# State-space mixer, groups 0 to 2: the clamped differences of the backward direction on VectorE instead of ScalarE

## Chip, core and metric

One Trainium2 chip, one NeuronCore. The metric is the device time of one execution in microseconds (us). The engines are TensorE (PE, with PEld for its weight loads), VectorE (DVE), ScalarE (ACT), GpSimd (POOL) and SyncE (SP), which issues the DMAs. Each engine works through its own instructions in order and waits on semaphores where it needs another's result.

## What is computed

Two layers of a diffusion backbone run for 128 prompt and 512 sample tokens. Layer 0 is attention with pooling, layer 1 a bidirectional Mamba-2 state-space mixer (SSD); each is followed by a gated MLP. The change lies in the mixer, whose diagonal part per chunk of 128 tokens, group of 8 heads and direction is

```
acs = cumsum(dt * a)                                  # per chunk and head
lmat = exp(where(lower, acs[i] - acs[j], -inf))       # 128 x 128 per head
wmat = (C_i . B_j) * lmat * dt[j]
y_diag = wmat @ x
```

The backward direction is the same on the flipped sequence. There are 4 groups, 5 chunks (one of the prompt, four of the sample) and 2 directions.

## The kernel before

All products are fp32. For the large projections each weight tile is cut into a rounded part and a rest by GpSimd (L940 makes `w_hi`, L944 makes `w_lo`, each as two instructions of 128x512), and TensorE makes three products of them with the two parts of the input (L974). The in-projection of the mixer is 40 such tiles (e0 to e39), ten to a group: B, C, four tiles of x, four of z. The scan's work is put between them by a list written out by hand, `SSD`, which every engine walks through in the same order, each doing its own part of every event. So an event's place in the list is its place in each engine's queue.

Per chunk the list holds, among others: `seg` (the decay matrices), `cb` (the product C.B, and on VectorE its masking, L2381, the scaled inputs `xdt`, L2389, and the multiplication into the decay matrices, L2395), `csf`/`csb` (states), `yo` (the part from the state; TensorE L1400, VectorE L2298, L2407, L2409) and `yd` (the diagonal product on TensorE, L1383 and L1388, gated by VectorE in L2401). The projection tile of e on ScalarE and VectorE is L1718, L2317, L2318, L1721 for B, C and x (a conv of three taps, then SiLU) and L1709 for z. L1749 copies transposed x tiles out of PSUM. PSUM banks 4 to 7 are handed round: the use number u of the list may begin on TensorE when the use u - 4 has been read by ScalarE or VectorE (`ssd_begin`).

`seg` of a chunk works in place on a row buffer `R` (or `R_mid`, in turn; in the last group `R_last`), [128, 2 directions, 8 heads, 128]. A DMA (L849) puts the row acs[i] of each head on all partitions; it is issued once the diagonal product two chunks earlier has used the buffer. ScalarE then makes max(acs[j] - acs[i], 0) head by head (L1767, eight instructions of 128x128), waits for them, and makes exp(-x) over the whole direction (L1770, one instruction of 128x1024), first direction 0, then direction 1. VectorE has no part in `seg`. Chunk n = 5g + c; the first three groups are n < N_MID = 15.

In each group the neighbourhood of the five `seg` events is, in every queue:

- chunk 0: behind csb of chunk 3, ahead of csb of chunk 2
- chunk 1: behind cb and csf of chunk 0, ahead of z tile e9 of the group and of yd of chunk 0; on ScalarE the copy-out of e9 (L1709) follows, for which VectorE's L2401 waits
- chunk 2: behind yd of chunk 1, ahead of the next group's C tile and yo of chunk 2
- chunk 3: behind the next group's first x tile, ahead of yd of chunk 2
- chunk 4: behind cb and csf of chunk 3, ahead of a copy-out of transposed x (L1749), of the next x tile, and of yd of chunk 3 and yo of chunk 4

Of the kernel before, what the change touches and what calls it, by code (L numbers as in the profile page):

```python
# [19 lines left out]
ALU = mybir.AluOpType  # L20
ACT = mybir.ActivationFunctionType
# [11 lines left out]
CHUNKS = 1 + NS // P  # L33
# [8 lines left out]
GH = 8  # L42
# [202 lines left out]
def build(nc, A, O):  # L245
    with ExitStack() as ctx:
# [140 lines left out]
        dt, acs, dec, wst, eacs = (a(n, [P, CHUNKS, 64]) for n in ("dt", "acs", "dec", "wst", "eacs"))  # L387
# [18 lines left out]
        N_MID, N_ALL = CHUNKS * (GROUPS - 1), CHUNKS * GROUPS  # L406

        def row_home(n):

            if n < N_MID:  # L410
                return (R, R_mid)[n % 2]
            return (R, R_last)[(n - N_MID) % 2]
# [5 lines left out]
        def rows_in(n, d_):  # L418

            if n < N_MID:  # L420
                return (R_in, RM_in)[n % 2][d_], 16 * (n // 2 + 1)
            i = n - N_MID
            return (RL_in[d_], 16 * (i // 2 + 1)) if i % 2 else (R_in[d_], 16 * (-(-N_MID // 2) + i // 2 + 1))
# [44 lines left out]
        def sem(name):  # L468
            return ctx.enter_context(nc.semaphore(name))
# [91 lines left out]
        xw_done = sem("xw_done")  # L561
        st_done = sem("st_done")
        seg_exp = sem("seg_exp")
        W_done = sem("W_done")
        y_done = sem("y_done")

# [887 lines left out]
        def _(act):  # L1454
            A_ = nc.scalar.activation
# [5 lines left out]
            for s_, name in enumerate(("c_ctx", "c")):  # L1461
                ins = A_(svec[:, :, s_], par[:, PARAM_AT[name]:PARAM_AT[name] + KD], ACT.Silu)
# [55 lines left out]
            for ev in ATT:  # L1518
                kind = ev[0]
                if kind == "mm":  # L1520
                    _, t, q = ev
                    if q == 3 and t < 12:
                        h, i = divmod(t, 3)
                        act.wait_ge(*acc_free(t))
                        buf = (q_raw, k_raw, v_raw)[i]
                        for s_, cols in SEGS:
                            ins = A_(buf[:, cols], buf[:, cols], ACT.Identity, bias=buf[:, NP_ + s_:NP_ + s_ + 1])
# [15 lines left out]
                elif kind == "S":  # L1543
                    _, h, j = ev
                    n = 5 * h + j
                    for c in range(2):
# [5 lines left out]
                        i = 24 + 2 * (j % 2) + c  # L1552
                        A_(prob[j % 2][:, c, 0:P if j == 0 else KEYS], src, ACT.Exp, bias=small[:, i:i + 1],
                           scale=SCALE, accum_out=small[:, i + 4:i + 5]).then_inc(att_free_act, 1)
                elif kind == "T":
                    _, h, j = ev
                    b = att_wait(ev)
                    n = CHUNKS if j else 1
# [105 lines left out]
            for k in range(KD):  # L1664
                act.wait_ge(t_done, k + 1)
                for s_, cols in SEGS:
                    ins = A_(h_hi[:, k, cols], tn[k % 2][:, cols], ACT.Identity, bias=modc(1, 0, k, s_))
# [29 lines left out]
            for ev in SSD:  # L1697
                kind = ev[0]
                if kind == "mm":
                    _, e, q = ev  # L1700
                    if q == 0:
                        continue
                    what, m = ssd_tile(e)
                    g, i = divmod(e, 10)
                    act.wait_ge(mm_done, T_E + e + 1)
                    if what == "z":
                        if e == 36:
                            act.wait_ge(ssd_mm, SSD_USE[("yd", GROUPS - 2, 3)] + 1)
                        A_(yg[:, m, :], acc(e % 2), ACT.Silu).then_inc(acc_free_act, 1)  # L1709
                        continue  # L1710
                    if i < 2 and g >= 2:
                        act.wait_ge(*ssd_end(("yd", g - 2, 4)))
                    if i == 2 and g:
                        act.wait_ge(*ssd_end(("trx", g - 1, 3, 1)))
                    if i > 2:
                        act.wait_ge(*ssd_end(("trx", g, i - 3, 1)))
                    buf = conv_buf(e)
                    A_(buf[:, :], acc(e % 2), ACT.Identity, bias=conv_row("ssd_conv_b", m),  # L1718
                       scale=conv_row("ssd_conv_w", 24 + m)).then_inc(conv_id, 1)
                    act.wait_ge(acc_free_dve, dve_accs(A_E + e))  # L1720
                    A_(buf[:, :], buf[:, :], ACT.Silu).then_inc(conv_silu, 1)  # L1721
                    continue
                g = ev[1]
                if kind == "ynorm":
                    y_high(ev[2])
                elif kind == "dtT":
                    act.wait_ge(dt_xb, 1)
                    step(A_(dt_e, dt_x, ACT.Abs))
                    step.wait()
                    A_(dt_e, dt_e, ACT.Exp, scale=-1.0).then_inc(dt_exp, 1)  # L1730
                elif kind == "acsT":
                    act.wait_ge(tot_w, 1)
                    A_(eacs[:, :, :], acs[:, :, :], ACT.Exp)
                    A_(dec[:, :, :], dec[:, :, :], ACT.Exp)
                    A_(wst[:, :, :], wst[:, :, :], ACT.Exp).then_inc(acs_exp, 1)
                    for i in range(2):
                        b = ssd_wait(ev + (i,))
                        A_(acsT[:, 512 * i:512 + 128 * i], bank(b, 512 - 384 * i)[0:64, :], ACT.Copy
                           ).then_inc(ssd_free_act, 1)
                elif kind in ("trB", "trx"):  # L1740
                    for i in range(2):
                        b = ssd_wait(ev + (i,))
                        cs = slice(1, CHUNKS) if i == 0 else slice(0, 1)
                        dst = b_tok[g % 2][:, cs, :] if kind == "trB" else \
                            x_tok[g % 2][:, cs, ev[2] * P:(ev[2] + 1) * P]
                        if g >= 2 and i == 0 and (kind == "trB" or ev[2] == 0):
                            act.wait_ge(*ssd_end(("yd", g - 2, 4)))
                            act.wait_ge(st_done, CS_AT[("csf", g - 2, 3)] + 1)
                        A_(dst, bank(b, P * (4 if i == 0 else 1)).rearrange("p (c n) -> p c n", n=P), ACT.Copy  # L1749
                           ).then_inc(ssd_free_act, 1)  # L1750
                elif kind == "init":
                    d_ = ev[2]
                    b = ssd_wait(ev)
                    if g:
                        act.wait_ge(ssd_mm, SSD_USE[("yo", g - 1, 4, 1)] + 1)
                    A_(st_f[1][:, :] if d_ == 0 else st_b[:, 3, :], bank(b), ACT.Copy).then_inc(ssd_free_act, 1)
                elif kind == "seg":
                    n = 5 * g + ev[2]
                    c = ev[2]


                    for d_ in range(2):
                        act.wait_ge(*rows_in(n, d_))
                        R_ = row_home(n)
                        for r in range(GH):
                            i = 32 * d_ + GH * g + r
                            ins = A_(R_[:, d_, r, :], R_[:, d_, r, :], ACT.Relu, bias=acs[:, c, i:i + 1], scale=-1.0)  # L1767
                        step(ins)
                        step.wait()
                        A_(R_[:, d_, :, :], R_[:, d_, :, :], ACT.Exp, scale=-1.0).then_inc(seg_exp, 1)  # L1770
                elif kind == "stT":
                    for d_ in range(2):
                        b = ssd_wait(ev + (d_,))
                        if g or d_:
                            act.wait_ge(st_stored, 16 * (2 * g + d_))
                        A_(st_out[:, :, :], bank(b).rearrange("p (q n) -> p q n", q=4), ACT.Copy
                           ).then_inc(ssd_free_act, 1)
# [9 lines left out]
            for hi, i, _, _, k0, k1 in H2_PADS:  # L1787
                ins = A_(hi[:, i:i + k1 - k0, PADS], mod[:, 72 + k0:72 + k1, :], ACT.Copy)
# [11 lines left out]
        def _(dve):  # L1800
            tt, ts, stt, cp = nc.vector.tensor_tensor, nc.vector.tensor_scalar, nc.vector.scalar_tensor_tensor, \
# [143 lines left out]
            for ev in ATT:  # L1945
                kind = ev[0]
                if kind == "mm":
# [4 lines left out]
                    if t < 12:  # L1952
                        h, i = divmod(t, 3)
# [11 lines left out]
                    else:  # L1965
# [10 lines left out]
                        for d_ in range(g + 1):  # L1976
                            r = 1 << d_ >> 1
# [60 lines left out]
                elif kind == "S":  # L2038
                    _, h, j = ev
                    for c in range(2):  # L2040
                        b = att_wait(ev + (c,))
                        src = bank(b, P) if j == 0 else bank(b, KEYS, 512 - KEYS // 2)
                        i = 24 + 2 * (j % 2) + c
# [5 lines left out]
                elif kind == "mix":  # L2049
                    _, h, j = ev  # L2050
                    n = P if j == 0 else KEYS
                    i = 28 + 2 * (j % 2)
# [23 lines left out]
                elif kind == "rbO":  # L2076
# [4 lines left out]
                    for s_, cols in RANGES:  # L2081
                        rbp = bank(b, P) if s_ == 0 else bank(b + 1)
                        ins = stt(o_nrm[:, cols], o_sb[:, cols], small[:, 22:23], rbp, ALU.mult, ALU.mult)
# [134 lines left out]
            for k in range(KD):  # L2218
                if k >= 2:
                    dve.wait_ge(*h_done(2, k - 2))  # L2220
                for s_, cols in RANGES:
                    rbp = bank(4, P) if s_ == 0 else bank(5)
                    ins = stt(tn[k % 2][:, cols], xT[:, k, cols], gain1[:, 2, k, s_:s_ + 1], rbp, ALU.mult, ALU.mult)
# [78 lines left out]
            for ev in SSD:  # L2302
                kind = ev[0]
                if kind == "mm":
# [4 lines left out]
                    g, i = divmod(e, 10)  # L2309
# [33 lines left out]
                    continue  # L2343
                if kind == "ynorm":
                    y_low(ev[2])
                if kind in ("ynorm", "yout", "seg"):
                    continue
                g = ev[1]
                c = ev[2] if len(ev) > 2 else 0
# [4 lines left out]
                elif kind in ("csb", "csf"):  # L2354
                    if kind == "csb" and c == 4:
                        dve.wait_ge(*ssd_end(("init", g, 1)))
                    d_ = 0 if kind == "csf" else 1
# [18 lines left out]
                elif kind == "cb":  # L2376
                    n = 5 * g + c
# [14 lines left out]
                    for d_ in range(2):  # L2392
                        dve.wait_ge(seg_exp, 2 * n + d_ + 1)
                        R_ = row_home(n)
# [7 lines left out]
                elif kind == "yo":  # L2402
                    y_ = y1[c % 2][:, :]
                    chain(skip_term(g, c))
                    for d_ in range(2):
# [3 lines left out]
                        ins = tt(y_, y_, y2[:, :], ALU.add)  # L2409
# [22 lines left out]
            for hi, i, lo, j, k0, k1 in H2_PADS:  # L2432
                ins = tt(lo[:, j:j + k1 - k0, PADS], mod[:, 72 + k0:72 + k1, :], f32(hi[:, i:i + k1 - k0, PADS]),
                         ALU.subtract)
                (step(ins) if k1 < 7 else ins.then_inc(shift_lo, 1))
            for m in range(KD):
                dve.wait_ge(mm_done, so_done(m))
                buf = tn[m % 2]
                for s_, cols in RANGES:
                    ins = stt(buf[:, cols], acc(so_slot(m))[:, cols], modc(1, 2, m, s_), rbs[:, cols], ALU.mult, ALU.mult)  # L2440
# [79 lines left out]
```

## Time and profile before

| | us |
|---|---|
| median of 3 runs | 2003.85 (2001.09 to 2008.55) |
| the profiled execution | 1999.62 |
| its span of instructions | 1997.7 |
| TensorE busy | 1864.4 (93%) |
| VectorE busy | 1032.1 (52%) |
| ScalarE busy | 605.8 (30%) |
| GpSimd busy | 1194.4 (60%) |
| mean granted TensorE clock | 0.977 of full |

The first three groups' scan lies between 960 and 1290 us of the span, one group to some 109.5 us, and the three look alike. The rows below are of the middle one, group 1, about 1075 to 1185 us. In a timeline, the first number is the start, the second the time taken by the x instructions that the row merges, and the bracket the engine's idle time just before with what ended it.

### The profile page before, as it was taken

What the parts mean: (1) busy time and instruction counts of PE and PEld (TensorE: products, weight loads), DVE (VectorE), ACT (ScalarE), POOL (GpSimd) and SP (SyncE); (2) the same over time, 40 slices, a digit from 0 to 9 for tenths busy, and PEclk for the clock granted to TensorE, in tenths of its full rate; (3) what the DMA queues carried; (4) which work ended last, traced back from release to release, by engine and by line L of the source; (5) the groups of instructions that cost most, each with busy time, mean ns of one, the idle gap of its engine ahead of it and who ended that gap; (6) DMA issues with size and microseconds to landing.
All of it is one profiled execution on the core that took longest, in us unless ns stands there. A gap on an engine that the chain in (4) does not pass through costs nothing. (4 is left out here: it accounts for less than half of the span.)

```text
span 1997.7 us, 33452 instructions
## 1 busy us (share of the span) xinstructions
PE 1864.4 (93%) x12857; PEld 1757.2 (88%) x12857; DVE 1032.1 (52%) x1608; ACT 605.8 (30%) x1152; POOL 1194.4 (60%) x869
## 2 busy tenths in 40 slices
PE   3988879999999999999999999987899999999997
PEld 2867768999999999989989898976899999999997
DVE  4545566466236515546565656578335632661553
ACT  4224322122002202223665555575112210220221
POOL 2423325777767777665645455532787777777764
PEclk9989989999999999999999999998999999999999
DMA  8631413342424333351523333222322222222212
GB/s 291 216 99 42 134 35 129 121 156 74 149 65 161 112 116 128 120 174 43 152 93 109 114 107 97 91 90 82 98 75 63 73 74 74 74 73 69 73 56 76
DMA packets 256187, 208.65 MB, mean 104 GB/s; under 512 B 7352, under 2 KB 235741, under 8 KB 255453
## 3 DMA queue, kind: packets, MB, share of 16 engines
q1 hardware_dynamic: 256093, 207.32, 32.9%
q8 instruction: 69, 1.13, 0.2%
q14 instruction: 25, 0.20, 0.0%
HBM read 196.63 MB, written 10.67 MB: 104 GB/s over the span
## 5 line engine op out<-in xcount | busy, mean ns | idle before, releaser
L940 POOL TENSOR_SCALAR w_hi<-raw 128x512 fp32r<-128x512 f32 (+1 forms) x432 | 644.9, 1510 | 778.1 <-PE ps L974 710.8
L944 POOL TENSOR_TENSOR w_lo<-raw,w_hi 128x512 fp32r<-128x512 f32 (+1 forms) x432 | 556.3, 1308 | 0.0
L974 PE MATMUL ps<-h_hi,w_hi 128*128 128x320 f32 (+1 forms) x1688 | 414.3, 326 | 4.7 <-DVE h_lo L2214 3.1
L974 PE MATMUL ps<-h_lo,w_hi 128*128 128x320 f32 (+1 forms) x1688 | 391.1, 312 | 0.0
L974 PE MATMUL ps<-h_hi,w_lo 128*128 128x320 f32 (+1 forms) x1688 | 389.9, 311 | 0.0
L974 PEld LDWEIGHTS ps<-h_hi,w_hi 128*128 128x128 f32 x1688 | 286.9, 192 | 27.2 <-issue 22.7
L974 PEld LDWEIGHTS ps<-h_hi,w_lo 128*128 128x128 f32 x1688 | 287.2, 190 | 0.0
L974 PEld LDWEIGHTS ps<-h_lo,w_hi 128*128 128x128 f32 x1688 | 286.9, 190 | 0.2 <-issue 0.2
L2109 DVE SCALAR_TENSOR_TENSOR xT<-ps,mod,xT 128x128 f32 (+1 forms) x112 | 56.5, 546 | 269.0 <-PE ps L974 263.3
L974 PE MATMUL ps<-g_hi,w_hi 128*128 128x322 f32 (+1 forms) x816 | 188.8, 313 | 7.0 <-DVE g_lo L2170 7.0
L974 PE MATMUL ps<-g_lo,w_hi 128*128 128x322 f32 (+1 forms) x816 | 187.5, 311 | 0.0
L974 PE MATMUL ps<-g_hi,w_lo 128*128 128x322 f32 (+1 forms) x816 | 187.1, 310 | 0.0
L1639 ACT ACTIVATE cg<-ps,small,par 128x130 f32<-128x130 f32 x88 | 49.8, 616 | 374.6 <-DVE small L2154 374.6
L974 PEld LDWEIGHTS ps<-g_hi,w_hi 128*128 128x128 f32 x816 | 137.1, 189 | 9.2 <-DVE g_lo L2170 7.8
L974 PEld LDWEIGHTS ps<-g_hi,w_lo 128*128 128x128 f32 x816 | 137.8, 189 | 0.0
L974 PEld LDWEIGHTS ps<-g_lo,w_hi 128*128 128x128 f32 x816 | 137.5, 189 | 0.0
L1892 DVE TENSOR_TENSOR ps<-ps,rbs 128x642 f32<-128x642 f32 x88 | 72.9, 829 | 85.1 <-PE ps L974 85.0
L1639 ACT ACTIVATE cv<-ps,small,par 128x130 f32<-128x130 f32 x88 | 49.7, 616 | 210.5 <-DVE small L2154 210.5
L974 PE MATMUL ps<-h_c,w_hi 128*128 128x322 f32 (+1 forms) x440 | 101.4, 312 | 0.0
L974 PE MATMUL ps<-h_b,w_hi 128*128 128x322 f32 x352 | 81.6, 314 | 0.0
L974 PE MATMUL ps<-h_b,w_lo 128*128 128x322 f32 x352 | 81.2, 312 | 0.0
L974 PE MATMUL ps<-y_hi,w_hi 128*128 128x322 f32 (+1 forms) x256 | 62.2, 325 | 17.8 <-POOL w_lo L944 17.8
(343 smaller groups left out, 2827.7 us busy)
## 6 DMA issues: line engine op xcount, KB each, us to landing
raw<-in_ffn_w_up SPq DMA_DIRECT2D x88, 512.0 KB, 3.8
ada<-in_ada_w SPq DMA_DIRECT2D x36, 1024.0 KB, 6.3
raw<-in_ssd_w_in SPq DMA_DIRECT2D x40, 512.0 KB, 4.0
raw<-in_ffn_w_down SPq DMA_DIRECT2D x32, 512.0 KB, 3.9
ada_att<-in_ada_w SPq DMA_DIRECT2D x12, 1024.0 KB, 8.3
R<-scr_acs SPq DMA_DIRECT2D x22, 512.0 KB, 5.6
raw<-in_att_w_in SPq DMA_DIRECT2D x16, 512.0 KB, 7.1
raw<-in_ssd_w_out SPq DMA_DIRECT2D x16, 512.0 KB, 4.0
```

The lines of the kernel that those rows point to most:

```text
L940: nc.gpsimd.tensor_scalar(w_hi[j % 2][:, a_:b_, :], raw[j][:, a_:b_, :], 1.0, None, ALU.mult).then_inc(w_hi_done, 1)
L944: ins = nc.gpsimd.tensor_tensor(w_lo[j % 2][:, a_:b_, :], raw[j][:, a_:b_, :], w_hi[j % 2][:, a_:b_, :].bitcast(F32), ALU.subtract)
L974: ins = mm(out[:, cols], w[slot][:, k, :], x[:, cols], start=first and k == 0 and i == 0, stop=last and k == n - 1 and i == 2)
L1639: ins = A_(buf[:, cols], acc(half)[:, cols], ACT.Identity, bias=small[:, b_:b_ + 1], scale=param_at(m + (wc + 44)))
L1892: step(tt(acc(slot), acc(slot), rrow(n)[:, :], ALU.mult))
L2109: ins = stt(x_, acc(slot)[:, cols], gate, x_, ALU.mult, ALU.add)
```

## The change

For n < N_MID, in direction 1 only, the eight clamped differences move from ScalarE to VectorE, as min(acs[i] - acs[j], 0), and ScalarE's exponential loses its scale of -1. VectorE makes them at the `seg` event's place in its own queue, after waiting for the row's DMA, and signals `seg_diff`; ScalarE waits for that ahead of its second exponential. Direction 0 and the last group are as before.

```diff
@@ scalar engine, kind == "seg"
                     for d_ in range(2):
                         act.wait_ge(*rows_in(n, d_))
                         R_ = row_home(n)
+                        if d_ and n < N_MID:
+                            act.wait_ge(seg_diff, n + 1)
+                            A_(R_[:, d_, :, :], R_[:, d_, :, :], ACT.Exp).then_inc(seg_exp, 1)
+                            continue
                         for r in range(GH):
                             i = 32 * d_ + GH * g + r
                             ins = A_(R_[:, d_, r, :], R_[:, d_, r, :], ACT.Relu, bias=acs[:, c, i:i + 1], scale=-1.0)
@@ vector engine
-                if kind in ("ynorm", "yout", "seg"):
+                if kind == "seg":
+                    n = CHUNKS * ev[1] + ev[2]
+                    if n < N_MID:
+                        dve.wait_ge(*rows_in(n, 1))
+                        R_ = row_home(n)
+                        for r in range(GH):
+                            i = 32 + GH * ev[1] + r
+                            ins = ts(R_[:, 1, r, :], R_[:, 1, r, :], acs[:, ev[2], i:i + 1], 0.0, ALU.subtract, ALU.min)
+                        ins.then_inc(seg_diff, 1)
+                    continue
+                if kind in ("ynorm", "yout"):
                     continue
```

## Rows read from the trace of the kernel before

**Rows 1.** The page: busy time, share of the span, number of instructions.

```profile
PE 1864.4 (93%) x12857; PEld 1757.2 (88%) x12857; DVE 1032.1 (52%) x1608; ACT 605.8 (30%) x1152; POOL 1194.4 (60%) x869
```

**Rows 2.** By stretch: busy PE, PEld, DVE, ACT, POOL; clock; DMA share; GB/s.

```profile
960.00:1290.00 330.00, 323.24 (x2299) 291.29 (x2298) 206.26 (x279) 195.19 (x390) 172.71 (x120) 0.98 0.36 110
```

**Rows 3.** Waits of TensorE, 1080 to 1190 us: total, times, longest.

```profile
PE ps L1375 <- DVE y L2407: 1.3, 1, 1.3
PE ps L1369 <- DVE y L2407: 1.0, 1, 1.0
```

**Rows 4.** Timeline of ScalarE, group 1, chunk 2.

```profile
1120.18 2.43 ACT L1767 ACTIVATE R_mid<-R_mid,acs 128x128 f32<-128x128 f32 x8
...
1123.61 0.87 ACT L1718 ACTIVATE cT<-ps,par 128x642 f32<-128x642 f32 x1
```

**Rows 5.** Timelines of VectorE, TensorE and GpSimd behind it.

```profile
1124.51 0.88 DVE L2317 SCALAR_TENSOR_TENSOR cT<-ps,par,cT 128x641 f32<-128x641 f32 x1 [6.40 <-ACT cT L1718]
...
1126.23 0.90 DVE L2298 TENSOR_TENSOR y<-x_tok,d_bc 128x512 f32<-128x512 f32 x1
...
1128.00 0.46 PE L1375 MATMUL ps<-cT,bT 128*128 128x128 f32 x2 [1.25 <-DVE y L2407]
...
1124.05 2.54 POOL L944 TENSOR_TENSOR w_lo<-raw,w_hi 128x512 fp32r<-128x512 f32 x2
```

**Rows 6.** Prices: a group of VectorE by form, then timelines of VectorE and GpSimd.

```profile
L2059 DVE TENSOR_SCALAR att<-prob,small 128x128 f32<-128x128 f32 x4 | 1.1, 279 | 0.0
...
917.65 2.95 POOL L940 TENSOR_SCALAR w_hi<-raw 128x512 fp32r<-128x512 f32 x2 [4.06 <-PE ps L974]
...
919.17 0.73 DVE L2252 TENSOR_SCALAR R<-R 128x320 f32<-128x320 f32 x1
...
922.25 1.31 DVE L2242 TENSOR_SCALAR R<-R 128x320 f32<-128x320 f32 x1
...
924.12 0.33 DVE L2242 TENSOR_SCALAR R<-R 128x320 f32<-128x320 f32 x1
```

**Rows 7.** The row buffer `R_mid`: its DMAs, issue to landing.

```profile
DMA to landing us min/median/max: 3.6/5.6/10.6
```

**Rows 8.** Timelines at chunks 0 and 3 of group 1: VectorE's idle time.

```profile
1085.38 0.90 DVE L2372 TENSOR_TENSOR y<-st_b,dec 128x512 f32<-128x512 f32 x1 [2.25 <-PE ps L1369]
...
1143.18 0.69 DVE L2401 TENSOR_TENSOR yg<-ps,yg 128x512 f32<-128x512 f32 x1 [3.80 <-PE ps L1388]
```

**Rows 9.** Timelines of ScalarE, VectorE and GpSimd at chunk 1 of group 1.

```profile
1094.65 1.07 ACT L1770 ACTIVATE R<-R 128x1024 f32<-128x1024 f32 x1
...
1098.09 1.06 ACT L1770 ACTIVATE R<-R 128x1024 f32<-128x1024 f32 x1
...
1100.46 0.71 ACT L1709 ACTIVATE yg<-ps 128x642 f32<-128x642 f32 x1
...
1098.65 0.06 DVE L2368 MEMSET small<- 128x1 f32 x1
...
1101.27 0.69 DVE L2401 TENSOR_TENSOR yg<-ps,yg 128x512 f32<-128x512 f32 x1 [2.56 <-ACT yg L1709]
...
1098.16 2.94 POOL L940 TENSOR_SCALAR w_hi<-raw 128x512 fp32r<-128x512 f32 x2 [3.01 <-PE ps L974]
```

**Rows 10.** The same engines and TensorE at chunk 4 of group 1.

```profile
1156.26 1.06 ACT L1770 ACTIVATE R_mid<-R_mid 128x1024 f32<-128x1024 f32 x1
...
1160.65 0.74 ACT L1749 ACTIVATE x_tok<-ps 128x512 f32<-128x512 f32 x2
...
1159.23 0.06 DVE L2375 MEMSET small<- 128x1 f32 x1
...
1161.43 1.02 PE L1400 MATMUL ps<-st_b,cT 128*128 128x512 f32 x2
...
1157.94 3.30 POOL L940 TENSOR_SCALAR w_hi<-raw 128x512 fp32r<-128x512 f32 x2 [2.32 <-PE ps L974]
...
1161.21 2.52 POOL L944 TENSOR_TENSOR w_lo<-raw,w_hi 128x512 fp32r<-128x512 f32 x2
```

More of the change, by code:

```diff
@@ L563, in build @@
         seg_exp = sem("seg_exp")
+        seg_diff = sem("seg_diff")
         W_done = sem("W_done")
```

## The prediction, made before the changed kernel was run

> **What bounds the kernel now.** The page first: TensorE is busy 93% of the span, the others 30 to 60% [rows 1]. So the question is what TensorE waits for where the change lies. The busy times by stretch say how much there is to win: in the 330 us of the three groups it works 323.24 us, idle 6.8 us in all [rows 2]. ScalarE is busy 195.19 of 330 us there, VectorE 206.26: neither is full, and VectorE, which gets the work, is the fuller one. The waits of TensorE in one group then say where the idle time is: two waits of 1.3 and 1.0 us, both for VectorE's L2407 [rows 3], and the same two stand in each group, 3 x 2.25 = 6.8 us, all of it. I call this place the seam. The timelines give the chain into it: ScalarE makes chunk 2's `seg`, direction 1's differences 1120.18 to 1122.61 among it, and only then begins the C tile at 1123.61 [rows 4]; VectorE, idle for 6.40 us, follows with L2317 at 1124.51, L2318, L2298, L2407, and TensorE, which needs the PSUM bank of L2407, starts at 1128.00 after 1.25 us of idling [rows 5]. Whoever reads no further expects 2.4 us off this chain and up to 2.25 us back per group.
>
> **What is removed.** Eight L1767 per chunk, 2.43 us [rows 4], 15 x 2.43 = 36 us of ScalarE's time. It counts only where TensorE waits for ScalarE. The SiLU and Exp tables are loaded as before: the differences of direction 0 and both exponentials remain.
>
> **What is added: the price.** Eight VectorE instructions of 128x128 per chunk, one input, a scalar per partition. The nearest row is L2059, same form, 279 ns [rows 6]; in the timeline such neighbours overlap by some 0.08 us, so I take 0.2 us each and 1.4 + 0.28 = 1.7 us for eight. GpSimd's splitting can hold them up. Of the same operation on 128x320, which takes 0.33 us alone (at 924.12), one takes 1.31 under a GpSimd L944 (at 922.25), and one 0.73 under an L940 (at 919.17) [rows 6]: an L944 instruction holds it for up to its own 1.27 us, half of its row of 2.54 for two [rows 5], an L940 for 0.40. From above: all eight held by 0.4 is 1.7 + 3.2 = 4.9 us and more if L944 joins. From below 1.7, since no row of this form is quicker than 279 ns; below nothing it can't be, for VectorE gives up no work. I take two holds per chunk where an L940 runs, 1.7 + 0.8 = 2.5 us, since most VectorE work under L940 goes at its own pace; both ends stay for the range. The Trainium skill, page "SBUF — State Buffer", section "Who interferes with whom", says that a VectorE instruction of this kind and a GpSimd instruction exclude each other for the whole instruction. The trace agrees for L944 and not for L940, where 0.40 us was waited of 1.47, half its row of 2.95 [rows 6].
>
> **What is added: the waits.** VectorE waits for the row's DMA. The load goes out after the diagonal product two chunks earlier and lands within 10.6 us [rows 7], and VectorE reaches `seg` 17 us or more after that product's end (least at chunk 4: 1142.1 to 1159.3); ScalarE never waited for it in these groups. Cost nothing; if a load came late, all of VectorE's queue would stand behind it. ScalarE waits for `seg_diff`, and behind that wait stands its next copy-out. This is what decides, so I go through the five places of a group, asking when VectorE gets there and when ScalarE wants the result (the end of its first exponential).
>
> Chunk 0: VectorE is there at 1082.5, and idles 2.25 us soon after [rows 8]; with L944 in the way the eight end at about 1086.6. ScalarE wants them at 1085.5, and is done at 1087.7 where it was done at 1089.0. Nothing behind it is hurt. Chunk 2: VectorE is there at 1118.1, inside its idle 6.40 us [rows 5], ScalarE at 1120.3. Hidden. Chunk 3: there at 1139.4, inside an idle 3.80 us [rows 8], wanted at 1144.9. Hidden, L944 included.
>
> Chunk 1: ScalarE's first exponential ends at 1095.72, but VectorE is there only at 1098.71, behind the previous chunk's L2395, L2289 and L2366 [rows 9]. ScalarE stands idle until VectorE has done, 1098.75 + 2.5 = 1101.2. Exponential 1.06, the table load in the 1.3 us between it and L1709, L1709 0.71: that ends at 1104.3, where it ended at 1101.17 [rows 9], and L2401 on VectorE, which waits for it, starts 3.1 us late. VectorE had some slack: 0.49 us idle ahead of L2381, and 0.58 us that L944 had cost it and no longer does. It loses 0.4 to an L940 later. The B tile's conv and SiLU ahead of chunk 2 come some 2.4 us late. That is just the 2.43 us which chunk 2's `seg` has lost on ScalarE: the C tile starts when it did, and **the seam stays**, 0 us. And small gains would not show: L2298 at 1126.23 already waits for L944's second instruction to end [rows 5], so the C tile must come 0.9 us earlier before any of it reaches TensorE. A loss does show, less 0.2 us.
>
> Chunk 4: ScalarE's first exponential ends at 1157.32, VectorE is there at 1159.29, under L940, with L944 from 1161.21 [rows 10]. Differences until 1159.3 + 2.5 = 1161.8, exponential until 1162.9; before, the copy-out L1749 behind it started at 1160.65, now at 1162.85, 2.2 us later. TensorE's L1400 at 1161.43 uses the PSUM bank that this copy-out frees at 1161.23 [rows 10]: slack 0.2. So **TensorE gets a new stall of 2.0 us**, once per group. What follows (the x tile, L2401, L2407) is late by 2.2 with TensorE late by 2.0, within the 0.3 us of slack that the next bank has; nothing gives the 2.0 back, since TensorE has no idle time until the next group's seam, whose chain hangs on TensorE itself.
>
> **The sum.** Seam 0, stall +2.0, three groups: +6 us. On the profiled execution 1999.62 + 6 = 2006; on the median, 4.2 above it, 2003.85 + 6 = 2010.
>
> **Rivals.**
> - Forecast, 0.58: 2010. Its own range: with one hold at chunk 4 the stall is 1.6 and the sum 5; with two holds and 0.4 us more in chunk 1, the seam adds 0.2. 2007 to 2013.
> - The last differences of chunk 4 fall behind L944, 0.17. Decides at 0.1 us: the eighth would start at about 1161.1 with one hold, L944 at 1161.21 [rows 10]. Then +1.25 per group on top, 3 x 3.3 = 10 us, and with 0.6 us of loss at the seam 2014 to 2016.
> - GpSimd holds nearly every difference, 0.12. One difference, one GpSimd instruction in turn: at chunk 4 three instructions (L940's second, both L944) of 1.5 + 2.5 us, so that the differences end at 1165.5, stall 5.6; at chunk 1 four of them, 4.2 us beyond my 1101.2, all of it at the seam. 3 x 9.8 = 29 us, 2033. For it: L944 does so [rows 6]. Against: L940 gave way after 0.40 us. This is what the quoted page's rule gives if it holds for L940 too.
> - Hidden after all, 0.08: VectorE reaches chunks 1 and 4 earlier than now, since its waits for ScalarE's conv tiles shorten. Against: it is the split at L944 and TensorE that set its time there. Time 2004.
> - Faster, 0.05: VectorE's part of chunk 1 comes no later than ScalarE wants it, 1095.7, that is 3 us earlier than its row shows; then the C tile gains its 2.43 us and the seam goes, 3 x 2.25 = 6.8 us, 1997; to decide for it, chunk 4 must be free too.
>
> **The numbers.** About 0.5% (10 us) is what a measurement of this kernel can tell from no change. Likeliest 2010. The range takes in the rival of L944 and the hidden case, and some of the way to the case of 2033, whose price can come in part: 2001 to 2022. Below 1993.8: 0.03. Above 2013.9: the rival of L944 mostly, the 2033 case, and a little of the forecast's upper end: 0.31. Within: 0.66.
>
> **What the changed profile would show.** ScalarE idle ahead of its second exponential in chunks 1 and 4 of each group, 5 and 4 us, released by VectorE's differences, and in no other chunk for over 1.5 us. A new wait of TensorE's L1400 for ScalarE's L1749, 2 us, once per group. The seam's two waits of 1.3 and 1.0 us still there. Eight differences in 1.7 us where no GpSimd instruction runs, 2.5 under L940. The stretch of the three groups 6 us longer, the rest unchanged. The forecast is wrong if the L1400 wait is absent, if the seam is gone, or if the differences take over 3.5 us.

## The result

The changed kernel takes 2016.28 us (median of 6 runs, 2013.01 to 2018.18) against 2003.39 us for the kernel before in the same comparison. The ratio is 1.0063, with a 95% interval of 1.0051 to 1.0076: slower by 10 to 15 us. The likeliest forecast was 2010, the range 2001 to 2022.

The page of the changed kernel, busy times, answers to [rows 1]:

```profile
PE 1872.8 (93%) x12857; PEld 1764.6 (88%) x12857; DVE 1074.1 (53%) x1728; ACT 570.3 (28%) x1032; POOL 1196.2 (59%) x869
```

ScalarE has lost 120 instructions and 35.5 us, VectorE has gained 120 and 42 us. TensorE has the same instructions and is busy 8.4 us longer, since some of its matmuls ran slower; only about 2 us of that lie in the three groups' scan, the rest in code ahead of it and behind it that is the same. Its waits in the stretch of one group (1080 to 1195 us; total, times, longest) answer to [rows 3]:

```profile
PE ps L1401 <- ACT x_tok L1750: 2.7, 1, 2.7
PE ps L1376 <- DVE y L2422: 1.3, 1, 1.3
PE ps L1370 <- DVE y L2422: 1.0, 1, 1.0
```

The two waits of the seam are untouched. The new one, TensorE's L1401 (L1400 before) for ScalarE's copy of transposed x (L1750, before L1749), stands in each of the three groups, 2.7 or 2.8 us. Chunk 4 of group 1 in the timelines of ScalarE, VectorE, TensorE and GpSimd, with the idle time ahead of an instruction in brackets, answers to [rows 10]:

```profile
1160.81 1.06 ACT L1775 ACTIVATE R_mid<-R_mid 128x1024 f32<-128x1024 f32 x1
1167.30 1.06 ACT L1768 ACTIVATE R_mid<-R_mid 128x1024 f32<-128x1024 f32 x1 [5.43 <-DVE R_mid L2358]
1168.27 0.75 ACT L1750 ACTIVATE x_tok<-ps 128x512 f32<-128x512 f32 x2
...
1163.74 0.66 DVE L2358 TENSOR_SCALAR R_mid<-R_mid,acs 128x128 f32<-128x128 f32 x1
1163.76 0.06 DVE L2390 MEMSET small<- 128x1 f32 x1
1163.94 3.27 DVE L2358 TENSOR_SCALAR R_mid<-R_mid,acs 128x128 f32<-128x128 f32 x7
...
1168.90 2.08 PE L1401 MATMUL ps<-st_b,cT 128*128 128x512 f32 x2 [2.75 <-ACT x_tok L1750]
1169.98 1.52 PE L975 MATMUL ps<-h_hi,w_hi 128*128 128x322 f32 x2
...
1162.49 3.37 POOL L941 TENSOR_SCALAR w_hi<-raw 128x512 fp32r<-128x512 f32 x2 [2.34 <-PE ps L975]
1165.84 2.51 POOL L945 TENSOR_TENSOR w_lo<-raw,w_hi 128x512 fp32r<-128x512 f32 x2
```

Read it in this order. ScalarE's first exponential ends at 1161.87. VectorE begins the differences only at 1163.74 and needs until 1167.21, 3.47 us, since it shares that time with both kinds of GpSimd's split instructions. ScalarE has idled for 5.43 us when it makes the second exponential, and its copy frees TensorE's bank 2.75 us too late. Then there is something that the waits don't list: the pair of L1401 that took 1.02 us before [rows 10] takes 2.08, and the next pair of the projection 1.52 where it took 0.85. That pair in the kernel before:

```profile
1161.89 0.85 PE L974 MATMUL ps<-h_hi,w_hi 128*128 128x322 f32 x2
```

The granted clock, in stretches laid about this spot, goes with it. Columns: stretch, its length, busy time of PE, PEld, DVE, ACT, POOL, then the clock, the DMA share and GB/s. First the kernel before, then the changed one, both from the start of that L1400 or L1401:

```profile
1161.40:1165.00 3.60, 3.60 (x22) 3.12 (x22) 2.55 (x4) 2.91 (x3) 2.33 (x2) 1.00 0.46 176
```

```profile
1168.90:1172.90 4.00, 4.00 (x13) 2.97 (x14) 2.84 (x4) 3.02 (x4) 0.00 (x0) 0.61 0.50 137
```

At a mean of 0.61, most of the 4 us went at the lower of TensorE's two levels, 1.2 GHz, after a pause of 2.75 us. Laying the two traces of TensorE side by side, instruction by instruction, the lag behind the kernel before grows by 2.9 us at the wait and by another 1.6 us over the matmuls behind it, 4.5 us at each chunk 4.

Some of it comes back at the seam, where the pause is as long as it was. The kernel before, then the changed one, on TensorE:

```profile
1129.45 2.04 PE L1369 MATMUL ps<-xw,b_tok 128*128 128x512 f32 x2 [0.99 <-DVE y L2407]
1131.29 1.77 PE L1406 MATMUL ps<-consts,st_p 128*128 128x128 f32 x8
```

```profile
1135.65 1.10 PE L1370 MATMUL ps<-xw,b_tok 128*128 128x512 f32 x2 [0.99 <-DVE y L2422]
1136.58 1.04 PE L1407 MATMUL ps<-consts,st_p 128*128 128x128 f32 x8
```

The kernel before ran these at the lower level, the changed one not, in groups 1 and 2: 1.6 and 1.4 us less. In all, the three groups' scan has become 3 x 4.5 - 3.0 = 10.5 us longer. The two profiled executions differ by 14.6 us; of the other 4.1, 1.7 had arisen before the scan and 2.2 arose in the last 60 us, in code that is the same. These last 2.2 us are no effect of the change: all of the traces below but that of chunk 1 alone show them too against this one trace of the kernel before, also those of kernels that take the same time as it. 10.5 alone lies inside the interval of the ratio.

### The profile page after: what moved, and what is told of

The parts are those of the page before. It is cut to its first block and busy times, and to the rows that moved or that the text cites. A ratio compares the mean times of both kernels' runs of the same rounds, so it can differ in the third digit from the quotient of the medians.

```text
span 2012.2 us, 33467 instructions
## 1 busy us (share of the span) xinstructions
PE 1872.8 (93%) x12857; PEld 1764.6 (88%) x12857; DVE 1074.1 (53%) x1728; ACT 570.3 (28%) x1032; POOL 1196.2 (59%) x869
## 5 line engine op out<-in xcount | busy, mean ns | idle before, releaser
L945 POOL TENSOR_TENSOR w_lo<-raw,w_hi 128x512 fp32r<-128x512 f32 (+1 forms) x432 | 556.3, 1309 | 0.0
```

What stands on the lines that cost most here:

```text
L945: ins = nc.gpsimd.tensor_tensor(w_lo[j % 2][:, a_:b_, :], raw[j][:, a_:b_, :], w_hi[j % 2][:, a_:b_, :].bitcast(F32), ALU.subtract)
```

## The experiments

All but the last vary in which chunks of a group get the new division of work, and where in VectorE's queue. They share one form: a list of chunks, and the differences in a function. In short, against the changed kernel:

```diff
+        ON_DVE = [n for n in range(N_ALL) if n < N_MID and n % CHUNKS in (0, 1, 2, 3)]
-                        if d_ and n < N_MID:
-                            act.wait_ge(seg_diff, n + 1)
+                        if d_ and n in ON_DVE:
+                            act.wait_ge(seg_diff, ON_DVE.index(n) + 1)
...
-                    if n < N_MID:
-                        ...
+                    if n in ON_DVE:
+                        differences(n)
```

The ratios are to the kernel before, run beside each of them.

### Chunks 0 to 3, and chunk 4 alone

The diff above is the first; in the second the list is (4,).

> VectorE makes the differences in chunks 0 to 3 of a group, ScalarE in chunk 4 as in the kernel before. Theory: the loss is the meeting at chunk 4, where VectorE comes late and TensorE waits 2.8 us per group and then goes on at half clock for some us. So here the time is that of the kernel before, 2002 to 2005 us, TensorE's wait for ScalarE's transposed x copy is gone, and the seam's two waits of 1.3 and 1.0 us are still there, since chunk 1 still gives back what chunk 2 saves. Rival: the loss is VectorE's 42 us of new work and its contest with GpSimd, spread over all chunks alike: four fifths of 10.6 us stay, about 2012 us.

> The opposite: VectorE makes the differences in chunk 4 alone. Theory: all of the loss is there, 10 to 13 us over the kernel before, 2013 to 2017 us, with the wait of 2.8 us per group and the slow clock behind it. Rival (spread work): a fifth of 10.6 us, about 2005.5 us.

Without chunk 4: 2002.98 us, ratio 0.9985 (0.9971 to 0.9999); the wait of L1401 is gone and TensorE's waits in the group are those of before:

```profile
PE ps L1377 <- DVE y L2439: 1.3, 1, 1.3
PE ps L1371 <- DVE y L2439: 1.0, 1, 1.0
```

Chunk 4 alone: 2019.77 us, ratio 1.0058 (1.0037 to 1.0078), at least as slow as the whole change, with one chunk in five. The median lies above the 2013 to 2017 that were expected, 16 us over that of the kernel before; the ratio makes it 7 to 16 us. Four chunks of work on VectorE cost nothing that can be measured (in the trace the scan is as long as before, to 0.1 us), one costs it all. The theory of work spread evenly falls.

The second one's wait is longer than in the changed kernel, which was not expected:

```profile
PE ps L1402 <- ACT x_tok L1751: 3.9, 1, 3.9
```

Its differences there took from 1171.83 to 1175.80, 3.98 us, two of them held behind GpSimd's second kind of split instruction and not one, and VectorE came to them 0.7 us later against TensorE. In this trace, of the slowest of seven executions, the three groups' scan is 19 us longer than before: 4 us of waiting at each chunk 4, and 1.6 to 2.7 us of slow matmuls behind it.

### Without chunk 1, and without chunks 1 and 4

The lists are (0, 2, 3, 4) and (0, 2, 3).

> All chunks but chunk 1. Theory: without the meeting at chunk 1 the conv of the B tile isn't late, chunk 2 is 2.4 us shorter on ScalarE, and the seam's waits of 2.3 us per group go (6.8 us in all, and with them what the clock loses behind them, 1 to 1.5 us per group), while the stall of chunk 4 stays: 10.6 less 7 to 11 us, 2003 to 2007 us. Rival (spread work): four fifths of 10.6 us, about 2012 us, seam unchanged.

> Chunks 0, 2 and 3 only. Theory: neither meeting hurts, and the seam is gone: 7 to 11 us under the kernel before, 1992 to 1997 us. Rival (spread work): three fifths of 10.6 us, about 2010 us. A third view, that GpSimd's split pins VectorE's L2303 at the seam whatever comes before it: no gain, 2003 us.

Without chunk 1: 2006.00 us, ratio 1.0002 (0.9984 to 1.0019). TensorE has one wait left in the group, that of chunk 4:

```profile
PE ps L1402 <- ACT x_tok L1751: 2.7, 1, 2.7
```

The seam is gone, and with it 2.4 us of waiting and, in these traces, 1.4 to 1.7 us of slow matmuls per group: 12.0 us for the three groups. Chunk 4 costs 12.2 us in them, so the two cancel here too.

This trace also shows that a pause of 2.75 us doesn't always bring the slow matmuls. It is as long in all three groups. From the start of the L1402 behind it, group 0 and group 1:

```profile
1054.65:1058.65 4.00, 4.00 (x12) 2.97 (x13) 2.84 (x4) 3.02 (x4) 0.00 (x0) 0.57 0.47 133
1164.90:1168.90 4.00, 4.00 (x23) 3.52 (x24) 2.84 (x4) 3.02 (x4) 0.00 (x0) 1.00 0.47 131
```

In group 1 the clock stays up, and the loss behind the pause is 0.1 us; in groups 0 and 2 it is 1.7 us each.

Without chunks 1 and 4 there is no wait of TensorE in the group at all, and the kernel takes 1993.30 us, ratio 0.9930 (0.9909 to 0.9951). This is the gain that a first look at the seam promises. The view that GpSimd's split pins VectorE there whatever comes falls: it would have hidden 0.9 us, and the gain on the chain was 2.4.

### Chunk 2 alone, and chunk 1 alone

The lists are (2,) and (1,).

> VectorE makes the differences of chunk 2 alone, one chunk in five. Theory: chunks 0 and 3 are hidden on both engines and chunk 2 carries all of the gain, so the time is that of the kernel with chunks 0, 2 and 3: 1992 to 1996 us, no wait of TensorE left in the three groups. Rival (ScalarE's relief counts wherever it falls): a third of that kernel's gain of some 10 us, 2000 us.

> Chunk 1 alone. Theory: ScalarE waits there for VectorE, the B tile's SiLU comes 2 to 2.5 us late, and with chunk 2 as in the kernel before nothing pays it back: the seam's idle time grows from 2.3 to 4.5 us per group, some 7 us and up to 2 us of slow clock on top: 2009 to 2013 us. Rival: VectorE's slack takes it up, and the seam stays because GpSimd's split pins it: 2003 us.

Chunk 2 alone: **1991.52 us, ratio 0.9939 (0.9927 to 0.9952)**, the same gain as with chunks 0, 2 and 3 within the intervals, so chunks 0 and 3 do nothing that these times can tell. (In the traces the scan with chunks 0, 2 and 3 is 1.3 us the shorter, 0.4 us at each chunk 4.) It beats both kernels. Its stretch of the three groups, to be laid beside [rows 2], and the meeting at chunk 2 on ScalarE and VectorE:

```profile
960.00:1290.00 330.00, 329.47 (x2371) 298.55 (x2370) 216.07 (x309) 190.33 (x371) 180.08 (x126) 1.00 0.37 113
```

```profile
1118.08 1.06 ACT L1776 ACTIVATE R_mid<-R_mid 128x1024 f32<-128x1024 f32 x1
1119.05 1.04 ACT L1769 ACTIVATE R_mid<-R_mid 128x1024 f32<-128x1024 f32 x1
1119.99 0.87 ACT L1720 ACTIVATE cT<-ps,par 128x642 f32<-128x642 f32 x1
...
1116.28 0.69 DVE L2433 TENSOR_TENSOR yg<-ps,yg 128x512 f32<-128x512 f32 x1 [2.62 <-PE ps L1390]
1116.89 1.65 DVE L2314 TENSOR_SCALAR R_mid<-R_mid,acs 128x128 f32<-128x128 f32 x8
```

TensorE is busy 329.47 of 330 us and the mean clock is 1.00. VectorE has the differences at 1118.54, ScalarE wants them at 1119.1, and doesn't stop between its two exponentials: a division of work that pays.

Chunk 1 alone: 2013.56 us, ratio 1.0060 (1.0043 to 1.0077), the seam's waits 3.3 and 0.7 us, 4.0 and not 2.3:

```profile
PE ps L1377 <- DVE y L2439: 3.3, 1, 3.3
PE ps L1371 <- DVE y L2439: 0.7, 1, 0.7
```

The median is just over the 2009 to 2013 expected, and the waiting a little less than the 4.5 us. In the trace the three seams account for 7.3 us of loss, waiting and slow matmuls together; the times say 9 to 15 us, and where the rest arises isn't shown. So chunk 1's meeting costs the B tile what chunk 2's shortening saves the C tile; in the changed kernel the two cancel.

### Chunk 4 one place earlier

All five chunks; chunk 4's differences stand ahead of the state update of chunk 3 (`csf`), no longer behind it. `early` makes the differences of chunk n if `EARLY` names this place for it.

```diff
+            EARLY = {4: 'csf'}
...
                 elif kind in ("csb", "csf"):
+                    if kind == "csf":
+                        early("csf", 5 * g + c + 1)
```

> All five chunks on VectorE, but chunk 4's differences one place earlier in VectorE's queue, ahead of the state update (csf of chunk 3) and not behind it: 1.4 us sooner. Theory: what counts is when VectorE gets there. ScalarE's copy comes 1.4 us sooner or so, but the state of chunk 4, which TensorE's first L1401 of chunk 4 needs 1.4 us after it was ready, is now late by the differences: the wait of 2.8 us becomes one of about 2 us and its releaser VectorE's state update, not ScalarE's copy. 2012 to 2015 us. Rival (the place in the queue is of no matter, the amount of work is): 2014 to 2016 us with ScalarE's copy as the releaser.

2003.27 us, ratio 1.0009 (0.9999 to 1.0018). Both the 2012 to 2015 expected and the rival's 2014 to 2016 are missed: no loss is left that the times can tell. VectorE and TensorE at chunk 4:

```profile
1157.00 2.62 DVE L2314 TENSOR_SCALAR R_mid<-R_mid,acs 128x128 f32<-128x128 f32 x8
1159.54 0.68 DVE L2402 TENSOR_TENSOR y<-st_f,dec 128x512 f32<-128x512 f32 x1
...
1161.17 1.10 PE L1402 MATMUL ps<-st_f,cT 128*128 128x512 f32 x2 [1.19 <-DVE small L2405]
1162.11 1.02 PE L1402 MATMUL ps<-st_b,cT 128*128 128x512 f32 x2
```

The releaser (L2405, which stands just behind the state update) is as foreseen. But the eight took 2.62 us: three of them were held under GpSimd's first kind of split instruction, none behind the second. So the wait is 1.2 us and not 2. And the matmuls behind it take 1.10 and 1.02 us, not 2.08: the clock stays up. Chunk 4 still costs 1.4 us per group; the seams of groups 1 and 2, where the clock stays up too, give 3.0 of these 4.2 us back. The same work on the same engine, a place earlier in the queue, made 11 us by the ratios and 13 by the medians.

### Half of the differences at chunk 4

```diff
-                        for r in range(GH):
+                        for r in range(GH // 2 if ev[2] == 4 else GH):
```

> The changed kernel with the differences of heads 4 to 7 left out in chunk 4 of direction 1 of the first three groups (those heads' decay matrices are not the reference's). It tells VectorE's late arrival at chunk 4 from the price of the eight instructions there, 3.5 us with GpSimd in the way. Theory: both are needed for the stall; with four of them, some 1.7 us, ScalarE's copy comes 1.8 us sooner and the wait of 2.8 us falls to about 1.0, below which the clock stays up: 2003 to 2008 us. Rival (arrival alone): the wait stays over 2 us, 2012 us or more.

The kernel leaves out the differences of heads 4 to 7 in chunk 4, direction 1. 2001.68 us, ratio 0.9996 (0.9987 to 1.0005), a little under the 2003 to 2008 expected; the wait is 0.8 us:

```profile
PE ps L1401 <- ACT x_tok L1750: 0.8, 1, 0.8
```

VectorE arrives as late as in the changed kernel, its four differences take 1.47 us, about what eight take undisturbed (1.65), and the loss is not there. So late arrival alone is not enough: the price under GpSimd is as much part of the cause. That a remaining wait of 0.8 us costs nothing measurable goes with two things in the trace: the clock stays up behind it, so that chunk 4 costs 1.0 us per group, and the seams' slow stretch is missing, here in all three groups, which gives 4.7 us back. That there is a length of wait below which the clock stays up, as the expectation has it, is not shown.

## Why the prediction was right, and where it was not

**The seam stays: right**, and for the reason given. The differences at chunk 1 end 2.22 us after they began (2.5 said), the successor of L2401 (L2416) starts 2.8 us late against TensorE (3.1 said), and the C tile starts 0.2 us earlier against TensorE than before. The changed kernel at chunk 1, ScalarE and VectorE, answers to [rows 9]:

```profile
1107.11 1.06 ACT L1768 ACTIVATE R<-R 128x1024 f32<-128x1024 f32 x1 [6.58 <-DVE R L2358]
...
1105.00 2.02 DVE L2358 TENSOR_SCALAR R<-R,acs 128x128 f32<-128x128 f32 x7
1110.29 0.69 DVE L2416 TENSOR_TENSOR yg<-ps,yg 128x512 f32<-128x512 f32 x1 [3.27 <-ACT yg L1710]
```

Chunk 1 alone and everything without chunk 1 show both halves of the cancellation.

**Chunks 0, 2 and 3 hidden: right**; leaving 0 and 3 out changes nothing that the times can tell. At chunk 0 ScalarE waits 0.98 us (1.1 said), without effect. The row's DMA never held VectorE.

**A new stall at chunk 4, once a group, through L1749's bank: right in place, too small in size.** Said 2.0 us, measured 2.7 to 2.8 in the waits and 2.9 in the lag. The term that failed is the price under GpSimd, 2.5 us; measured 3.47, just short of the 3.5 us that the prediction named as a sign of being wrong. The undisturbed price was near, 1.7 said, 1.65 measured. I took two holds of 0.4; there were three under L940, and the last difference fell behind L944, as the second rival has it, on a margin of 0.1 us that the forecast put on the other side: it was issued when L944 had run for 0.1 us, and took 1.28 us.

**The clock behind the stall: not in the sum.** 1.6 us per group, 4.8 us in all, less the 3.0 us that the seams of groups 1 and 2 gave back, for a reason that stays open. The trace showed both levels at the seam of the kernel before, where a pair of 128x512 matmuls takes 2.04 us after a pause of 0.99 us and another 1.02 us where there was none; the forecast counted a wait as its own length only. With 3 x 2.9 = 8.7 for the stall and 1.8 net for the clock the sum is 10.5, where 6 was said.

So the mechanism was right and two terms of the sum were off. The medians differ by 12.9 us, twice the 6 of the sum; the range holds the result because it was drawn wide enough for the L944 rival, not because of the sum. That rival, 2014 to 2016 us, had the time almost, by some luck, and its mechanism half: the L944 hold did come, but its stall of 3.3 us was 2.9, the loss at the seam did not come, and the clock, which it did not have either, made up for both. The rival of GpSimd holding nearly every difference (2033) fell: at chunk 4 three were held by about 0.35 us and one by 1.0. By the Trainium skill ("SBUF — State Buffer", section "Who interferes with whom") a VectorE instruction of such a kind and one of GpSimd keep each other out for their whole length; the trace agrees for L944 and its successor L945, where the hold was as long as that instruction had left, and not for L940, where it was some 0.35 us. The rival "faster" was right in what it asked for: take chunk 1 and chunk 4 out of the way, and 1993.3 us is what is left, or 1991.5 with chunk 2 alone.

## What to carry to other kernels

Before a part of a step is handed to another engine, ask at each place when that engine gets there in its own queue and when the first wants the result. Busy shares say nothing on it: ScalarE, 28% busy, stood idle for 6.6 and 5.4 us at two of five places of each group. Hand over only the part that stands on the bound engine's chain; here one chunk in five made the whole gain of 0.6%, two made a loss, and two were of no use. And count a stall of TensorE not by its length alone, but with the slow matmuls that may follow it; whether they come is not fixed by its length.

## What the hardware showed that was not expected

- A pause of TensorE of 2.75 us was followed by 1.6 us of loss at the lower clock in each group of the changed kernel, and in two groups of three, by 1.7 us, in the kernel without chunk 1. In its third one, with the same pause at the same place, the loss was 0.1 us (granted clock 1.00). Pauses of 1.2 and 0.8 us there were followed by none. But the seam's pauses of 1.3 and 1.0 us, the same in the kernel before and the changed one, were followed by slow matmuls in the one and not in the other, in groups 1 and 2; with half of the differences at chunk 4 in no group. So the length of the pause alone doesn't decide it. What does stays open; no run varied it alone.
- Eight VectorE differences of 128x128 take 1.65 us alone, and 2.22, 2.62, 3.47 or 3.98 us beside GpSimd's split, for the same instructions. At chunk 4, VectorE coming 0.7 us later against TensorE moved the price from 3.47 to 3.98 us.
